# Turns one step later, finer steps beside the latent pieces, and a semaphore of its own for the high halves of the weight ring

## The chip, the cores and the metric

One NeuronCore of a Trainium2 chip runs the whole program. The metric is the device time of one execution in microseconds, the median of several runs. A text that gives a place in time gives it in us from the span's start in the profiled execution.

## The reference, cut to what matters

Two transformer blocks run one after the other over 256 tokens of width 2048, in float32.

```
first_block:
  n1 = rms_norm(x);  proj = n1 @ w_in            # q_lat 512, kv_lat 256, k_pe 64, q/k/v of the window attention
  q  = rms_norm(q_lat) @ w_q_b                   # 8 heads x (128 plain + 64 rotated columns)
  kv = rms_norm(kv_lat) @ w_kv_b                 # 8 heads x (128 key + 128 value columns)
  q, k = rms_norm per head, rope on the last 64; o_mla = causal softmax attention
  o_swa = window attention, 16 heads, bias table and a sink per head
  h = x + concat(rms_norm(o_mla), rms_norm(o_swa)) @ w_out
  h = h + peer(...)                              # routing over 16384 experts, peer_u, peer_v
second_block:
  proj = rms_norm(x) @ w_in_2                    # 6 x 1024 columns for two attentions, 4096 for gates
  oa = differential attention (4 heads), on = neighbourhood attention (8 heads, bias, 256 keys)
  x = x + rms_norm((g_a * oa @ w_a + g_b * on @ w_b) @ w_out)
  u = relu(rms_norm(x) @ w_up)^2                 # 2048 -> 8192
  x = x + rms_norm(u @ w_down)                   # 8192 -> 2048
```

## The kernel before, in words

**Pieces.** All weights come as 1101 pieces of 128 x 1024 float32 (512 KB), in the fixed order of the list `order`. SyncE's queue loads piece m into one of NR = 5 slots of `raw` (L2744). ScalarE writes its rounded high half to one of NH = 3 slots of `whi` (L1868), VectorE the rest to `wlo` (L2100). TensorE multiplies with high and low halves. A high slot may be overwritten when `piece_used` (s_used) says that TensorE is through with the whole piece, high and low products both; VectorE's low split waits for the high split alone and so for the same event through it. The split of piece n+2 is issued on both engines ahead of the products of piece n.

**Three forms of product.** `gemm` / `gemm_piece` (L340, L1655): 12 matmuls of 512 columns in a piece, weights moving: eight with `whi`, four with `wlo`. With `mid=True` the piece is cut into two halves of six, and a step (below) is taken between them. `gemm_rows` (L360, L1679) does the last three pieces of a product row block by row block. `gemm_wide` / `wide_piece` (L389, L1698), used by peer_w_q, peer_u and w_up: eight matmuls of 512 columns with `whi` stationary, then eight of 256 columns with `wlo`.

**Steps.** One Python program (`walk`) is run once for every engine and gives each engine its instructions in one fixed order. Side work (norms, rotations, turns by TensorE, attention units) stands in generators in `tasks` and `idle`; `step()` advances every one of them to its next `yield`. A generator that yields between two actions puts the second one behind the next piece, or half piece, on every engine. Each engine works strictly through its own order, so an instruction that waits holds up all behind it.

**Latent pieces.** After the fifth block of w_in come, in this order: `keys(0)`, `keys(1)` (one piece each), `swa_queries(1)` (eight pieces of w_in), `queries(2)` (the rotated part of q, two pieces), `values(0)`, `values(1)` (one each), `queries(0)`, `queries(1)` (two each). Their side work: `k_nope` (squares on ScalarE, `k_scale` and four `k_rows` on VectorE, turns, splits of the turned tile), `q_side` (norm of the window queries and their turns), `k_rope`, `q_nope`, `q_rope`, `q_scale`. `evac2` empties a product with half on ScalarE and half on VectorE. After `queries(1)` steps are taken with no product beside them until all turned tiles are split; then the scores of the latent attention start. GpSimd's order there: two fillings with zero for `k_rope` (L2680; the second waits for turns of the first), and, behind `queries(1)`, one small fill and eight writes of 2 MB that clear scr_g (L2694). Later in that order stands the reload of x into R (L2685), which the first residual behind w_out reads.

**Attention units.** `attend` is one unit: scores, yield, maximum and exponential, yield, turns of the exponentials (they wait for ScalarE's exponential, L1914), yield, copy, yield, product with the values, yield, finish. The window attention's 12 units run beside the first half of w_out, one started every second step, at half pieces; the neighbourhood attention's 8 units run beside the gate columns of w_in_2, two at a time, at whole pieces, and `finish_idle` behind the fifth gate product takes what steps are left over.

Of the kernel before, what the change touches and what calls it, by code (L numbers as in the profile page):

```python
# [37 lines left out]
def build(nc, D, out):  # L38
# [12 lines left out]
    with ExitStack() as ctx:  # L51
# [144 lines left out]
        s_hi, s_lo, s_used = sem("hi_split"), sem("lo_split"), sem("piece_used")  # L196
        s_vec = sem("vector_step")

        def walk(steps):
# [189 lines left out]
            def gemm_wide(name, units, both, toks, post, lead=2):  # L389
                taken = [take(accs) for _ in units]  # L390
                for c in range(4):
                    while len(toks) < min(2 * c + lead, 8):
                        step(0)
                    for n, (u, (pair, free)) in enumerate(zip(units, taken)):
                        i, low = piece(name, 4 * u + c)
                        high = fresh("PE", (s_hi, i + 1))
                        b = [banks[2 * pair], banks[2 * pair + 1]]
                        go("mm_wide", i, b, c, both, high, low, fresh("PE", toks[2 * c:2 * c + 2], free))
                        last = used_up()
                        if c == 3:  # L400
# [105 lines left out]
            def attend(scores, U, nk, scale, sink, pslots, blocks, pv, finish, combine=None, per_head=None, added=None):  # L506
# [30 lines left out]
                yield  # L537
# [227 lines left out]
            def swa_unit(t, h0):  # L765
# [20 lines left out]
                return attend(scores, U, nk, 1.0, sinks[:, h0:h0 + U], psw, 4, pv, finish, added=(of_head, bias_done[-1:]))  # L786
# [25 lines left out]
            def q_rope(ts, te, j):  # L812
                tr = []
                for t in range(2):
                    x = heads(ts[:, t, :], 8)
                    a = yield from squares(x, 8, ssq[:, 1, t, :], te)
                    t_ssq.append(a)
                    go("gain_rows", x, gq, 8, fresh("DVE", a, t_gr))
                    a = up("DVE", "gained")
                    yield  # L820
                    tr.append(rope(ts[:, t, :].rearrange("p (u c h) -> p u c h", u=8, c=2), 8, 32, CS[:, 0, t], CS[:, 1, t],
                                   [a, t_rope, x_read], Y[:, 0, 1024:2048]))
                    yield
# [6 lines left out]
            def q_scale():  # L830
                while len(t_ssq) < 6:
                    yield
                yield
# [51 lines left out]
            def keys(j):  # L885
                pair, b, last = gemm("w_kv_b", j, 2, BH[:, 4:6, :], BL[:, 4:6, :], nKV)
# [5 lines left out]
            def values(j):  # L892
                pair, b, last = gemm("w_kv_b", 2 + j, 2, BH[:, 4:6, :], BL[:, 4:6, :], nKV)
# [4 lines left out]
            def queries(j):  # L898
                pair, b, last = gemm("w_q_b", 2 * j, 4, BH, BL, nQ)
# [449 lines left out]
            def na_unit(h):  # L1349
# [16 lines left out]
                def masked_first():  # L1366
# [5 lines left out]
                                             masked))  # L1372
# [274 lines left out]
        def tensor_program(e):  # L1647
# [7 lines left out]
            def gemm_piece(i, b, c, n, lh, ll, high, low, free, kks=(0, 1)):  # L1655
# [5 lines left out]
                for kk in kks:  # L1661
                    kt = 2 * c + kk
                    w = slice(512 * kk, 512 * kk + 512)
                    for t in range(2):
                        a = slice(128 * t, 128 * t + 128)
                        mm(b[t][:, :], lh[:, kt, a], whi[:, s, w], kt == 0, False)
                        mm(b[t][:, :], ll[:, kt, a], whi[:, s, w], False, False)
# [11 lines left out]
            def gemm_rows(held, t, b, n, lh, ll, free):  # L1679
# [3 lines left out]
                for i, c, split in held:  # L1683
# [3 lines left out]
                    for kk in range(2):  # L1687
# [3 lines left out]
                        mm(b[t][:, :], lh[:, kt, a], wlo[:, s, w], False, False)  # L1691
                        last = mm(b[t][:, :], ll[:, kt, a], whi[:, s, w], False, kt == 2 * n - 1)
                    if t == 1:
                        last.then_inc(s_used, 1)
# [3 lines left out]
            def wide_piece(i, b, c, both, high, low, free):  # L1698
                s = i % NH
                for mark in free:  # L1700
                    e.wait_ge(*mark)
                for mark in high:
                    e.wait_ge(*mark)
                for kk in range(4):
                    kt = 4 * c + kk
                    x = both[:, kt, :, :].rearrange("p a n -> p (a n)")
                    for m in range(2):
                        w = slice(256 * kk + 128 * m, 256 * kk + 128 * m + 128)
# [1186 lines left out]
```

## Time and profile before

| | us |
|---|---|
| median of 3 runs | 3256.81 |
| lowest and highest | 3256.42 and 3257.52 |
| the profiled execution's own time | 3259.14 |
| its span, first to last instruction | 3257.3 |
| TensorE busy in matmuls | 3200.2 |
| VectorE busy | 2106.2 |
| ScalarE busy | 1517.7 |
| GpSimd busy | 492.0 |

Busy times are sums over the span. The granted clock of TensorE over the span was 0.994 of full. The profile's idle time before an instruction comes with what ended it; only waits on the chain to the end cost time.

### The profile page before, as it was taken

The numbers are of one execution on the slowest core, as the hardware profiler recorded it, in microseconds if no ns is written. First come the engines' busy times: TensorE is split into PE (matmuls) and PEld (weight loads), VectorE is DVE, ScalarE is ACT, GpSimd is POOL, SyncE is SP. The second block draws the span as 40 slices with busy tenths as digits, with TensorE's granted clock in tenths as the row PEclk, the third lists the DMA queues.
The fourth block names the chain that finished last, engine by engine and source line by source line (L and its number), as shares of the span: only waits on it lengthen the run. The fifth ranks groups of instructions, "written<-read, shape, count | busy, mean of one in ns | idle before, by whom it ended". The sixth has DMA issues, their size and how long they took to land.

```text
span 3257.3 us, 40800 instructions
## 1 busy us (share of the span) xinstructions
PE 3200.2 (98%) x16112; PEld 2715.7 (83%) x16112; DVE 2106.2 (65%) x3062; ACT 1517.7 (47%) x2006; POOL 492.0 (15%) x322
## 2 busy tenths in 40 slices
PE   8989999999999999999999999999999999999998
PEld 7788888888888888888888888888888788888886
DVE  6766578887555576666666565565465655655556
ACT  5645454545444444444444544445444544444443
POOL 1000005777777200000000000000000000000000
PEclk9999999999999999999999999999999999999999
DMA  8623557888888866666665555444555455555554
GB/s 321 252 85 130 181 183 208 214 214 215 212 214 211 262 249 244 250 248 245 245 233 200 197 184 174 165 170 176 191 194 188 174 192 191 193 189 193 189 192 149
DMA packets 220286, 660.95 MB, mean 203 GB/s; under 512 B 56704, under 2 KB 56848, under 8 KB 217536
## 3 DMA queue, kind: packets, MB, share of 16 engines
q1 hardware_dynamic: 170864, 600.81, 52.9%
q0 software_dynamic: 49232, 57.54, 8.7%
q8 instruction: 127, 2.08, 0.3%
q14 instruction: 63, 0.52, 0.0%
HBM read 622.48 MB, written 35.78 MB: 202 GB/s over the span
## 4 chain that ended last, share of the span: by engine, by line
PE 90%; DVE 6%; ACT 2%; issue 1%; DMA 1%; DVEq 0%; ACTq 0%; SPq 0%
PE PS L1649 89%; DVE wlo L2102 2%; PE PS L1723 2%; ACT whi L1872 1%; DMA raw<-in_w_in_b 0%; DVE R L2606 0%; ACT M L1914 0%; DVE AA L2148 0%; ACT Y L1958 0%; DVE TMP L2177 0%; DVE M L2507 0%; DVE TMP L2178 0%; DVE BB L2148 0%; DMA R<-in_x 0%; DMA M<-in_na_bias 0%
## 5 line engine op out<-in xcount | busy, mean ns | idle before, releaser
L2102 DVE TENSOR_TENSOR wlo<-raw,whi 128x1024 fp32r<-128x1024 f32 x1101 | 1343.8, 1224 | 889.6 <-ACT whi L1872 878.4
L1872 ACT ACTIVATE whi<-raw 128x1024 fp32r<-128x1024 f32 x1101 | 1157.8, 1057 | 1033.4 <-PE PS L1649 998.3
L1649 PE MATMUL PS<-whi,AA 128*128 128x512 f32 (+1 forms) x2880 | 718.7, 390 | 2.0 <-DVE AA L2148 1.2
L1649 PE MATMUL PS<-whi,BB 128*128 128x512 f32 x2640 | 667.4, 393 | 1.7 <-DVE wlo L2102 1.2
L1649 PEld LDWEIGHTS PS<-whi,AA 128*128 128x128 f32 x2880 | 537.0, 189 | 112.4 <-DVE AA L2148 2.0
L1649 PE MATMUL PS<-BB,whi 128*128 128x512 f32 x2304 | 577.4, 392 | 1.7 <-DVE BB L2148 1.7
L1649 PEld LDWEIGHTS PS<-whi,BB 128*128 128x128 f32 x2640 | 491.1, 188 | 102.3 <-DVE wlo L2102 1.8
L2699 POOL DMA_INDIRECT scr_g<-M x256 | 446.9, 1746 | 426.4 <-issue 390.2
L1649 PEld LDWEIGHTS PS<-BB,whi 128*128 128x128 f32 x2304 | 414.4, 189 | 76.1 <-DVE BB L2148 1.9
L1649 PE MATMUL PS<-wlo,AA 128*128 128x512 f32 (+1 forms) x1440 | 389.4, 388 | 1.9 <-DVE wlo L2102 1.9
L1649 PE MATMUL PS<-wlo,BB 128*128 128x512 f32 x1320 | 356.3, 389 | 0.5 <-DVE wlo L2102 0.5
L1649 PEld LDWEIGHTS PS<-BB,wlo 128*128 128x128 f32 x2304 | 314.3, 190 | 22.5
L1649 PE MATMUL PS<-BB,wlo 128*128 128x256 f32 x2304 | 321.2, 282 | 0.0
L1649 PEld LDWEIGHTS PS<-wlo,AA 128*128 128x128 f32 x1440 | 271.2, 188 | 58.0 <-DVE wlo L2102 2.3
L1649 PEld LDWEIGHTS PS<-wlo,BB 128*128 128x128 f32 x1320 | 247.7, 188 | 53.1 <-DVE wlo L2102 0.9
L1649 PE MATMUL PS<-AA,whi 128*128 128x512 f32 (+1 forms) x1056 | 263.8, 391 | 2.6 <-DVE AA L2148 2.2
L1649 PEld LDWEIGHTS PS<-AA,whi 128*128 128x128 f32 (+1 forms) x1056 | 189.4, 188 | 37.2 <-DVE AA L2148 2.8
L1649 PEld LDWEIGHTS PS<-AA,wlo 128*128 128x128 f32 (+1 forms) x1040 | 141.8, 189 | 10.0
L1649 PE MATMUL PS<-AA,wlo 128*128 128x256 f32 (+1 forms) x1040 | 147.2, 282 | 0.0
L1857 ACT ACTIVATE AA<-M 128x512 fp32r<-128x512 f32 x72 | 45.5, 632 | 150.8 <-DVE M L2507 143.8
L1857 ACT ACTIVATE M<-TMP 128x512 f32<-128x512 f32 x64 | 40.5, 633 | 128.1 <-DVE TMP L2498 100.5
L2708 POOL DMA_DIRECT2D M<-scr_a x16 | 8.8, 547 | 589.8 <-DVE AA L2514 543.6
(236 smaller groups left out, 1570.0 us busy)
## 6 DMA issues: line engine op xcount, KB each, us to landing
raw<-in_peer_u SPq DMA_DIRECT2D x256, 512.0 KB
raw<-in_peer_v SPq DMA_DIRECT2D x256, 512.0 KB
raw<-in_w_in SPq DMA_DIRECT2D x160, 512.0 KB
raw<-in_w_up SPq DMA_DIRECT2D x128, 512.0 KB
raw<-in_w_down SPq DMA_DIRECT2D x128, 512.0 KB
raw<-in_w_out SPq DMA_DIRECT2D x64, 512.0 KB
raw<-in_w_in_a SPq DMA_DIRECT2D x32, 512.0 KB
scr_g<-M POOLq DMA_DIRECT2D x8, 2048.0 KB, 30.1
```

The lines of the kernel that those rows point to most:

```text
L1649: return e.matmul(outp, l, r, start=start, stop=stop)
L1723: last = e.transpose(banks[bank][:, 128 * n:128 * n + 128], s, ident)
L1857: e.activation(o, x, func, **kw).then_inc(sem(name), 1)
L1872: e.activation(whi[:, n % NH, :], raw[:, n % NR, :], ACT.Copy).then_inc(s_hi, 1)
L2102: e.tensor_tensor(wlo[:, n % NH, :], raw[:, n % NR, :], bf(whi[:, n % NH, :]), ALU.subtract).then_inc(s_lo, 1)
L2699: e.indirect_dma_start(out=D["scr_g"].rearrange("e (t o) -> (e t) o", o=1), out_offset=bass.IndirectOffsetOnAxis(ap=EID[t][:, k:k + 1], ax ...
L2708: e.dma_start(glt[i], D["scr_a"][sc, :, :]).then_inc(sem(f"gelu_fetched{i}"), 16)
```

## The change

Five edits:

- The ring: a new semaphore `piece_hi_used` is raised at the last product with a high half. ScalarE's split of piece n now waits for it and for the low split of piece n-3 (which read that high half), no more for `piece_used`. VectorE's low split now waits for `piece_used` itself. In `gemm_rows`, `kpe_mm` and `sub_scores` the product with `wlo` becomes the last of its three.
- w_up alone, where one unit of 256 columns is computed at a time (60 pairs of pieces): two pieces are held, 16 high products and then 16 low ones. The first group, two units interleaved, stays at one piece.
- `keys`, `values`, `queries` use `mid=True`, so a step is also taken in the middle of each of their ten pieces.
- `q_rope`: both squares first, then both gains and both rotations in one step, and the turns in the next. `q_scale` waits for all turned q tiles.
- `slack=1` in the window and the neighbourhood attention: one more `yield` between the exponential and its turns.

```
-        s_hi, s_lo, s_used = sem("hi_split"), sem("lo_split"), sem("piece_used")
+        s_hi, s_lo = sem("hi_split"), sem("lo_split")
+        s_hi_used, s_used = sem("piece_hi_used"), sem("piece_used")
...
             def gemm_wide(name, units, both, toks, post, lead=2):
-                for c in range(4):
-                    while len(toks) < min(2 * c + lead, 8):
+                at_once = 2 if len(units) == 1 and name in ('w_up',) else 1
+                for c0 in range(0, 4, at_once):
+                    while len(toks) < min(2 * (c0 + at_once - 1) + lead, 8):
                         step(0)
                     for n, (u, (pair, free)) in enumerate(zip(units, taken)):
-                        i, low = piece(name, 4 * u + c)
-                        go("mm_wide", i, b, c, both, high, low, fresh("PE", toks[2 * c:2 * c + 2], free))
+                        held = []
+                        for c in range(c0, c0 + at_once):
+                            i, low = piece(name, 4 * u + c, NH - 1 - (c - c0))
+                            held.append((i, c, fresh("PE", (s_hi, i + 1)), low, fresh("PE", toks[2 * c:2 * c + 2], free)))
+                        go("mm_wide", held, [banks[2 * pair], banks[2 * pair + 1]], both)
+                        for _ in held[1:]:
+                            last = up("PE", "piece_used")
+                            step()
                         last = used_up()
...
-            def attend(..., per_head=None, added=None):
+            def attend(..., per_head=None, added=None, slack=0):
...
-                yield
+                for _ in range(1 + slack):
+                    yield
                 bank, bfree = yield from wait_for(misc)
                 tk = transposed(...)
...
             def q_rope(ts, te, j):
-                tr = []
+                xs, ta, tr = [heads(ts[:, t, :], 8) for t in range(2)], [], []
                 for t in range(2):
-                    x = heads(ts[:, t, :], 8)
-                    a = yield from squares(x, 8, ssq[:, 1, t, :], te)
-                    t_ssq.append(a)
-                    go("gain_rows", x, gq, 8, fresh("DVE", a, t_gr))
-                    a = up("DVE", "gained")
-                    yield
-                    tr.append(rope(...))
-                    yield
+                    ta.append((yield from squares(xs[t], 8, ssq[:, 1, t, :], te)))
+                t_ssq.extend(ta)
+                for t in range(2):
+                    go("gain_rows", xs[t], gq, 8, fresh("DVE", ta[t], t_gr))
+                    tr.append(up("DVE", "gained"))
+                for t in range(2):
+                    tr[t] = rope(...)
+                yield
...
             def q_scale():
-                while len(t_ssq) < 6:
-                    yield
-                yield
+                while len(t_ssq) < 6 or len(qt_done) < 6:
+                    yield
...
-                pair, b, last = gemm("w_kv_b", j, 2, BH[:, 4:6, :], BL[:, 4:6, :], nKV)
+                pair, b, last = gemm("w_kv_b", j, 2, BH[:, 4:6, :], BL[:, 4:6, :], nKV, mid=True)   # values, queries alike
...
             def split(n):                                   # ScalarE
                 if n >= NH:
-                    e.wait_ge(s_used, n - NH + 1)
+                    e.wait_ge(s_lo, n - NH + 1)
+                    e.wait_ge(s_hi_used, n - NH + 1)
...
             def split(n):                                   # VectorE
                 e.wait_ge(s_hi, n + 1)
+                if n >= NH:
+                    e.wait_ge(s_used, n - NH + 1)
```

## Rows read from the trace of the kernel before

**Rows 1.** The page's waits, whole span: engine, line, awaited; us in total, times, longest.

```profile
PE PS L1723 <- ACT M L1914: 8.6, 7, 2.9
```

**Rows 2.** Windows: stretch, busy time of the five engines, granted clock, DMA share, GB/s.

```profile
40.00:117.00 77.00, 73.26 (x356) 59.71 (x354) 55.91 (x114) 41.58 (x86) 9.05 (x8) 1.00 0.98 371
92.80:150.60 57.80, 55.50 (x257) 43.83 (x255) 46.45 (x97) 40.11 (x117) 1.12 (x1) 1.00 0.67 245
150.60:167.00 16.40, 6.48 (x33) 5.97 (x33) 13.95 (x35) 10.59 (x39) 0.95 (x1) 0.75 0.30 102
160.00:200.00 40.00, 35.80 (x284) 35.56 (x283) 24.67 (x56) 15.12 (x45) 0.00 (x0) 0.89 0.03 9
232.00:237.00 5.00, 5.00 (x19) 4.42 (x19) 4.89 (x18) 0.72 (x1) 0.00 (x0) 0.50 0.24 86
```

**Rows 3.** Groups of VectorE, 92 to 167 us: busy us, mean ns; idle before them.

```profile
L2102 DVE TENSOR_TENSOR wlo<-raw,whi 128x1024 fp32r<-128x1024 f32 x19 | 23.0, 1221 | 9.7 <-ACT whi L1872 9.7
L2190 DVE TENSOR_SCALAR M<-PS,ST 128x512 f32<-128x512 f32 x5 | 3.7, 746 | 0.1
```

**Rows 4.** Group of ScalarE, the same stretch and columns.

```profile
L1958 ACT ACTIVATE Y<-M 128x128 f32<-128x128 f32 (+1 forms) x50 | 13.8, 285 | 6.3 <-issue 6.3
```

**Rows 5.** Timeline of VectorE, 123 to 139 us: start, us, instructions, [idle before].

```profile
123.60 0.75 DVE L2190 TENSOR_SCALAR R<-PS,ST 128x512 f32<-128x512 f32 x1 [0.81 <-PE PS L1649]
...
138.44 0.75 DVE L2355 TENSOR_TENSOR M<-M,ST 128x256 f32<-128x256 f32 x2
```

**Rows 6.** Timeline of TensorE, 139 to 168 us.

```profile
139.25 0.66 PE L1723 MATMUL PS<-C,M 128*128 128x128 f32 x4 [0.37 <-DVE M L2355]
...
153.96 0.66 PE L1723 MATMUL PS<-C,M 128*128 128x128 f32 x4 [3.32 <-DVE M L2182]
...
157.02 5.78 PE L1723 MATMUL PS<-C,M 128*128 128x128 f32 x28 [2.40 <-DVE M L2355]
...
167.00 1.01 PE L1649 MATMUL PS<-BB,AA 128*128 128x256 f32 x3 [4.20 <-DVE AA L2148]
```

**Rows 7.** Timeline of GpSimd, 0 to 470 us.

```profile
39.93 8.00 POOL L2694 DMA_DIRECT2D scr_g<-M  x7 [0.30 <-POOL M L2688]
105.00 1.12 POOL L2694 DMA_DIRECT2D scr_g<-M  x1 [57.07 <-issue]
154.68 0.95 POOL L2680 MEMSET M<- 128x1024 f32 x1 [48.56 <-PE PS L1723]
212.57 0.73 POOL L2685 DMA_DIRECT2D R<-in_x  x1 [56.95 <-DVE AA L2148]
```

**Rows 8.** DMA issues, 200 to 240 us: count, KB each, us from issue to landing.

```profile
R<-in_x POOLq DMA_DIRECT2D x1, 2048.0 KB, 9.9
```

**Rows 9.** Timeline of VectorE, 231 to 234 us.

```profile
232.28 1.41 DVE L2373 SCALAR_TENSOR_TENSOR R<-PS,ST,R 128x512 f32<-128x512 f32 x2
```

**Rows 10.** TensorE's waits, 205 to 284 us (window attention).

```profile
PE PS L1723 <- ACT M L1914: 6.6, 4, 2.9
```

**Rows 11.** TensorE's waits, 2173 to 2280 us (neighbourhood attention), and its last turns.

```profile
PE PS L1723 <- ACT M L1914: 2.0, 3, 0.8
2278.62 0.60 PE L1723 MATMUL PS<-C,Y 128*128 128x128 f32 x4
```

**Rows 12.** TensorE's waits, 2535 to 2553 us (start of w_up); ScalarE's timeline there.

```profile
PE PS L1723 <- DVE R L2606: 1.3, 2, 0.9
PE PS L1649 <- DVE AA L2148: 0.4, 1, 0.4
2547.39 1.06 ACT L1872 ACTIVATE whi<-raw 128x1024 fp32r<-128x1024 f32 x1 [1.72 <-PE PS L1649]
```

**Rows 13.** Timeline of TensorE: a piece of w_up, then a part of one of w_down.

```profile
2707.28 2.00 PE L1649 MATMUL PS<-AA,whi 128*128 128x512 f32 x8
2709.12 1.11 PE L1649 MATMUL PS<-AA,wlo 128*128 128x256 f32 x8
...
3227.47 1.98 PE L1649 MATMUL PS<-whi,BB 128*128 128x512 f32 x8
```

More of the change, by code:

```diff
@@ L504, in walk, with attend @@
             alt = [0]
-            def attend(scores, U, nk, scale, sink, pslots, blocks, pv, finish, combine=None, per_head=None, added=None):
+            def attend(scores, U, nk, scale, sink, pslots, blocks, pv, finish, combine=None, per_head=None, added=None, slack=0):
                 bank, bfree = yield from wait_for(misc)
@@ L898, in queries @@
             def queries(j):
-                pair, b, last = gemm("w_q_b", 2 * j, 4, BH, BL, nQ)
+                pair, b, last = gemm("w_q_b", 2 * j, 4, BH, BL, nQ, mid=True)
                 ts, free = take(qrows)
@@ L1696, in gemm_rows, with wide_pieces @@
                     last.then_inc(sem("rows_done"), 1)
[L1698 to L1708, printed above, removed]
-                        mm(b[m][:, :], whi[:, s, w], x, kt == 0, False)
-                for mark in low:
-                    e.wait_ge(*mark)
-                for kk in range(4):
-                    kt = 4 * c + kk
-                    for m in range(2):
-                        w = slice(256 * kk + 128 * m, 256 * kk + 128 * m + 128)
-                        last = mm(b[m][:, 0:256], wlo[:, s, w], both[:, kt, 0, :], False, kt == 15)
-                last.then_inc(s_used, 1)
+            def wide_pieces(held, b, both):
+                for i, c, high, low, free in held:
+                    for mark in free:
+                        e.wait_ge(*mark)
+                    for mark in high:
+                        e.wait_ge(*mark)
+                    for kk in range(4):
+                        kt = 4 * c + kk
+                        x = both[:, kt, :, :].rearrange("p a n -> p (a n)")
+                        for m in range(2):
+                            w = slice(256 * kk + 128 * m, 256 * kk + 128 * m + 128)
+                            last = mm(b[m][:, :], whi[:, i % NH, w], x, kt == 0, False)
+                    last.then_inc(s_hi_used, 1)
+                for i, c, high, low, free in held:
+                    for mark in low:
+                        e.wait_ge(*mark)
+                    for kk in range(4):
+                        kt = 4 * c + kk
+                        for m in range(2):
+                            w = slice(256 * kk + 128 * m, 256 * kk + 128 * m + 128)
+                            last = mm(b[m][:, 0:256], wlo[:, i % NH, w], both[:, kt, 0, :], False, kt == 15)
+                    last.then_inc(s_used, 1)
             def transpose(srcs, bank, ready):
@@ L1742, in kpe_mm @@
                     mm(o, whi[:, s, w], AH[:, kt, :], kt == 0, False)
-                    mm(o, wlo[:, s, w], AH[:, kt, :], False, False)
-                    last = mm(o, whi[:, s, w], AL[:, kt, :], False, kt == 15)
+                    high = mm(o, whi[:, s, w], AL[:, kt, :], False, False)
+                    last = mm(o, wlo[:, s, w], AH[:, kt, :], False, kt == 15)
+                high.then_inc(s_hi_used, 1)
                 last.then_inc(s_used, 1)
@@ L1812, in sub_scores @@
                     mm(o, AH[:, hp, a], whi[:, s, w], True, False)
-                    mm(o, AH[:, hp, a], wlo[:, s, w], False, False)
-                    last = mm(o, AL[:, hp, a], whi[:, s, w], False, True)
+                    high = mm(o, AL[:, hp, a], whi[:, s, w], False, False)
+                    last = mm(o, AH[:, hp, a], wlo[:, s, w], False, True)
+                if end:
+                    high.then_inc(s_hi_used, 1)
                 last.then_inc(s_used if end else sem("sub_scores"), 1)
```

25 lines of the change are left out of this document (13 added, 12 removed).

## The prediction

> **What bounds the kernel now.** I read the page's busy times first: TensorE 3200 of 3257 us, so all its idle time together is 57 us, and no cut in the other engines' work counts unless TensorE waits for it there. Then the page's waits: the largest that this change touches is TensorE's turns waiting for ScalarE's exponentials, 8.6 us in all [rows 1]. Then windows, to see which stretch is dense. In 92.8 to 150.6 us TensorE is busy 55.5 of 57.8 us, in 150.6 to 167.0 only 6.48 of 16.4 [rows 2]: 12.2 us idle in the latent stage, the largest hole near the changed lines. VectorE is busy 46.45 + 13.95 = 60.4 of those 74.2 us, and 9.7 of the other 13.8 are waits of the low split for the high split [rows 3]; it has about 4 us of slack of its own. The clock belongs to the picture: it was granted 1.00 up to 150.6, 0.75 behind, and exactly half (1.2 of 2.4 GHz) in 232 to 237 [rows 2], behind a wait of 2.9 us [rows 10], so a hole costs more than its length. Last, the waits of each later stretch one by one.
>
> **1. Steps in the middle of the ten latent pieces, and q_rope's new order.** The products are the same; ten more steps draw the side work ahead. VectorE's order up to `head_scale` hardly shrinks: before it ran from the evacuation of the last window query product at 123.60 to `head_scale` at 138.44 [rows 5], 14.8 us, with TensorE's turns right behind at 139.25, having waited 0.37 [rows 6]. In the new order I count between the same two, by durations of this stretch: two evacuations .75 + .7 [rows 3], two low splits at 1.15 net of overlap, two gain-and-rope groups 2.1, x's low halves 1.7, the head sums 1.15, the root 2.1, the spread .75, the scale 1.15, and 1.05 of waiting: 13.7 us. It starts later, at 124.4 instead of 123.3, because both turn groups of the keys now stand behind one half piece and wait for all four `k_rows` (+1.1). So the scaled tile is there at 138.1. TensorE's work up to the turns is now two pieces (5.5), turns (.95) and one of values (2.75), which ends at 133.5: it waits 4.6.
>
> Then the q turns. `q_rope` gave them six steps behind the first squares; now both rotations stand in one step and the turns in the next, half a piece on. VectorE has to do a low split (1.15) that waits for ScalarE's squares (1.9; 16 of the groups of .28 [rows 4] beside evacuations) and high split (1.06), with 1.85 idle, then gains 1.3 and rotations 4.4: done at 147.6. TensorE is there at 140.5: it waits 7.1. The next spread and the k turns cost 2.7, and the drain before the latent scores keeps its 4.2 [rows 6]. Sum of waits 1.1 + 4.6 + 7.1 + 2.7 + 4.2 = 19.7 against 12.2 now: **+7.5**, the half clock of the holes taken as hidden in the waits for VectorE. Bounds: if VectorE's total is the only limit, holes move and none is added (0, and -2 if the earlier work thins the drain); if each of the new holes drops the clock as that of 2.9 us did, five us at half rate more, +12.
>
> The order also moves GpSimd. Its second zero fill was issued at 154.68, behind clears issued from 39.93 on, the last at 105.00 after 57 us in the queue [rows 7]. In the new walk the second fill, which waits for turns, is emitted ahead of the clears. So the eight writes leave near 155. In 40 to 117 us the DMA engines were busy .98 at 371 GB/s; in 160 to 200, .03 [rows 2]. Early pieces land sooner, worth 0.3 us by the one wait there (range 0 to 0.5): **-0.3**. But the reload of x was issued at 212.57 [rows 7] and took 9.9 us [rows 8] with the queue empty; the first scaled residual reads it at 232.28 [rows 9]. The clears took 77 us beside the weight pieces (39.9 to 117); with nearly nothing beside them I take 65 to 70, ending near 225, and the reload near 234, about when it is needed: **+0.5**, range 0 to 9.
>
> **2. One more step in the window attention.** Queued behind a waiting turn is all of TensorE's order. In 205 to 284 us TensorE waits 6.6 us for exponentials in four places [rows 10]. Half a piece (1.5 us) more between them: the three short ones vanish, the longest shrinks to nothing as well, as the units start every second step and the turns then fall on the other one. A wait of .8 for a low split there goes too. The half clock in 232 to 237 [rows 2] did 5 us in what full clock does in 2.5; its cause is that wait, so 2.6 come back. At the end of the half the pipeline drains one step later: the residual's 1.4 [rows 9] and a step without product, +1.8. Sum -6.6 - .8 - 2.6 + 1.8 = **-8.2**; range -6 (clock falls elsewhere) to -11 (drain hidden).
>
> **3. One more step in the neighbourhood attention.** Three waits, 2.0 us [rows 11], vanish behind a whole piece. A pair of units takes 8 steps instead of 7; over four pairs the last turns (now at 2278.62, .60 for a group) fall into the steps behind the fifth gate product. They are the same work in another place, with nothing late in front: **-2.0**, range -2.0 to 0 (two more unproductive steps of copies and exponentials).
>
> **4. The ring's semaphore.** In steady stages TensorE does not wait for splits at all, so there it is worth 0. It tells where VectorE is late. At the start of w_up ScalarE's high split begins at 2547.39, 1.72 idle, released by TensorE's last product of the older piece [rows 12]; with high products first that event comes some .95 us earlier. VectorE's low split then is done before the norm's turns need VectorE, and the waits of 1.3 + .4 [rows 12] go: **-1.7**, range 0 to -2.2. The added wait stands on VectorE's low split for `piece_used`; ahead of it was the same event by way of ScalarE, so nothing behind it comes later. The other added wait, ScalarE's for the low split of three pieces ago, is long met.
>
> **5. Pairs in w_up.** 60 pairs, the same matmuls, half the changes of form. Eight high products run from 2707.28 to 2709.12 in w_up, 1.84 us, against 1.81 for the same in w_down (3227.47 to 3229.28) [rows 13]. The .03 fits a cost of changing form; of it I take .02 a pair: 60 x .02 = **-1.2**, range -1.8 to 0 (a gain for nothing else would need a wait, and there is none). A pair holds two slots of `whi` of three: the third is split while 16 high products run (3.7 us against 1.06), so it costs nothing; with that cover gone it would be 1 us a pair.
>
> [...]
>
> **Sum.** -0.3 + 7.5 + 0.5 - 8.2 - 2.0 - 1.7 - 1.2 = -5.4. The profiled execution took 3259.1 (span 3257.3); its change is laid on the median, 2.3 us lower: 3256.8 - 5.4 = **3251.4**.
>
> **The rivals.**
>
> A. The latent stage loses nothing. For it: VectorE is the bound there (60.4 busy of 74.2), its work is the same, and TensorE's finer steps may only trade the final 4.2 and the 3.32 for waits ahead. Against: VectorE's idle time behind the high split (9.7) grows if ScalarE does squares first. Time: 3256.8 - 5.4 - 7.5 = 3243.9.
>
> B. Slower than before, by one mechanism: the reload of x behind the clears. If these keep the 77 us that they took, 155 + 2 + 77 = 234, the reload lands at 244, 9 us behind the first residual at some 235; VectorE stands, TensorE's next split stands, and the clock falls for 5 us (2.6 to 3.4). Price 12.4 in place of .5: 3251.4 + 11.9 = 3263.3. It decides from a landing at about 241, where the sum passes 0. Against: fewer other transfers than in 40 to 117, where pieces of 512 KB shared the engines.
>
> C. The ring and the pairs do nothing, which is what they say only on paper: TensorE never waits for either in steady state. Without the 1.7 and the 1.2: 3254.3.
>
> **How the numbers follow.** Forecast .50, A .30, B .10, C .10. A measurement of this kernel tells 0.2% (6.5 us) from no change, so the bounds are 3250.3 and 3263.3. The forecast's own spread, 3247 to 3257, lies for a third beyond 3250.3; A all; C none; B half above 3263.3, to which I add the upper ends of the latent term. Faster .30 + .17 = .47, slower .09, same .44. Range: A with its latent -2 at 3242 below, above the forecast with its latent term at +12 and a small share of B, 3260.
>
> **What would show it.** Right: TensorE's latent scores start at about 173 instead of 167.0, with a wait of some 7 us for the rotations in the middle of values(1) and one of 4 to 5 for the scale near 134; GpSimd's clears issued behind 155 and a DMA share near 1 until 225; no wait for exponentials in 205 to 284 and 2173 to 2280, granted clock 1.0 at 232 to 237; 16 high products of w_up in about 3.66 us; no waits at 2540 to 2551. Wrong: latent scores at or before 167 (A), the first residual waiting for x (B), any steady stage with waits for `whi` or `wlo`.

## The result, and the profile after

| | before | after |
|---|---|---|
| median | 3257.2 us (8 runs) | 3269.5 us (8 runs) |
| lowest and highest | 3256.4 and 3263.0 | 3263.7 and 3270.9 |
| profiled execution, its span | 3259.1, 3257.3 | 3267.9, 3266.0 |

Ratio 1.0032, 95% interval 1.0024 to 1.0041: slower by some 12 us where 5.4 us less were forecast. The profiled execution is one of the milder ones, 8.7 us over that of before.

The page of the changed kernel, busy times (part 1) and the chain of waits by engine (part 4):

```profile
PE 3200.5 (98%) x16112; PEld 2719.2 (83%) x16112; DVE 2093.6 (64%) x3062; ACT 1519.2 (47%) x2006; POOL 526.8 (16%) x322
...
PE 72%; POOL 14%; issue 4%; DVE 4%; DMA 3%; ACT 2%; DVEq 0%; ACTq 0%; SPq 0%; POOLq 0%
```

TensorE and ScalarE have their old sums. GpSimd has 35 us more (492.0 before), with the same number of instructions, and it stands in the chain to the end with 14%. The prediction says nothing of what this engine does behind the reload of x.

TensorE's waits over the whole span (line and awaited; us, times, longest). Lines have moved: the turns are L1734 (L1723 before), the products L1655 (L1649).

```profile
PE PS L1655 <- DVE AA L2165: 9.5, 5, 5.6
PE PS L1655 <- ACT whi L1887: 7.4, 3, 6.9
...
PE PS L1734 <- DVE M L2199: 5.7, 1, 5.7
...
PE PS L1734 <- DVE R L2183: 4.2, 1, 4.2
PE PS L1655 <- ACT PTb L1871: 3.8, 1, 3.8
PE PS L1734 <- DVE M L2372: 2.6, 1, 2.6
```

The exponentials of [rows 1] (8.6 us) are gone from the list altogether. New are the high split (6.9 at once), the rotations (5.7), the scale (4.2) and a copy by ScalarE (3.8). Their places, in TensorE's timeline:

```profile
133.40 1.97 PE L1734 MATMUL PS<-C,R 128*128 128x128 f32 x8 [4.19 <-DVE R L2183]
...
143.06 1.11 PE L1734 MATMUL PS<-C,M 128*128 128x128 f32 x4 [5.75 <-DVE M L2199]
...
158.94 0.66 PE L1734 MATMUL PS<-C,M 128*128 128x128 f32 x4 [2.56 <-DVE M L2372]
...
171.71 1.01 PE L1655 MATMUL PS<-BB,AA 128*128 128x256 f32 x3 [5.59 <-DVE AA L2165]
...
238.59 1.76 PE L1655 MATMUL PS<-M,PTb 128*128 128x64 f32 x8 [3.76 <-ACT PTb L1871]
...
1156.98 3.70 PE L1655 MATMUL PS<-BB,whi 128*128 128x512 f32 x8 [6.94 <-ACT whi L1887]
```

The first four answer to [rows 6]: the latent scores start at 171.7 instead of 167.0. The last stands at a piece of peer_u, the fifth from its end, where before TensorE had no wait at all. What held it, from the waits of 1140 to 1165 us:

```profile
DVE M L2524 <- DMA M<-scr_g: 10.1, 1, 10.1
```

VectorE stood 10.1 us for the gate values' load from scr_g, which it multiplies into peer_v's first operand. ScalarE's rounding of that operand waited for VectorE, and the high split of a piece of peer_u stood behind it on ScalarE:

```profile
1155.35 0.63 ACT L1871 ACTIVATE AA<-M 128x512 fp32r<-128x512 f32 x1 [12.11 <-DVE M L2524]
1155.88 1.04 ACT L1887 ACTIVATE whi<-raw 128x1024 fp32r<-128x1024 f32 x1
```

The load could only be issued when GpSimd had written all gate values into scr_g, 256 indirect writes. Windows (busy time of the five engines, granted clock, DMA share, GB/s), the first around that wait, the second to be held against the fourth of [rows 2]:

```profile
1150.00:1160.00 10.00, 3.06 (x8) 2.45 (x8) 3.95 (x7) 2.72 (x4) 0.00 (x0) 0.68 0.87 318
...
160.00:200.00 40.00, 34.41 (x257) 33.20 (x256) 21.42 (x49) 17.55 (x62) 3.18 (x3) 0.87 1.01 350
```

With the wait of 6.9 and the half clock behind it, VectorE's low split of the next piece comes 16.0 us later than before (1156.96 against 1140.93), where the last one ahead of the wait came 5.9 later (1143.27 against 1137.39): 10.1 us. The third column of the table below has the same 10 us. GpSimd's timeline has the clears where they were forecast, and the reload waiting behind them:

```profile
155.20 7.98 POOL L2711 DMA_DIRECT2D scr_g<-M  x7 [0.30 <-POOL M L2705]
207.44 1.12 POOL L2711 DMA_DIRECT2D scr_g<-M  x1 [44.26 <-issue]
218.34 0.72 POOL L2702 DMA_DIRECT2D R<-in_x  x1 [9.77 <-DMA scr_g<-M]
```

Lengths of four stretches, from TensorE's timelines, in us: from the start to the latent scores; from there to the wait at peer_w_q's start; from there to the norm ahead of w_up; and w_up and w_down, from w_up's first product to the wait at 3236.8 of before (the norm's 9 us between the last two are left out; they are the same in all). Each row is one profiled execution. The first column varies by up to 1.6 us between kernels that are the same up to that point (164.8 to 166.4 in experiments 6, 9 to 12 and 14).

| | to the scores | window attention | peer, second block | w_up, w_down |
|---|---|---|---|---|
| before | 167.0 | 181.2 | 2173.9 | 705.2 |
| after | 171.7 | 182.4 | 2179.7 | 702.2 |
| ring alone | 165.5 | 180.8 | 2173.0 | 704.2 |
| old ring in peer_u | 170.8 | 185.8 | 2169.6 | 703.1 |
| the same, early clears | 172.6 | 179.4 | 2169.6 | 703.0 |
| the same, latent edits undone | 165.6 | 180.0 | 2169.6 | 703.1 |

### The profile page after: what moved, and what is told of

Read it like the earlier page. It is cut to its first block, busy times and chain, and to the rows that moved or that the text cites. A ratio compares the mean times of both kernels' runs of the same rounds, so it can differ in the third digit from the quotient of the medians.

```text
span 3266.0 us, 41894 instructions
## 1 busy us (share of the span) xinstructions
PE 3200.5 (98%) x16112; PEld 2719.2 (83%) x16112; DVE 2093.6 (64%) x3062; ACT 1519.2 (47%) x2006; POOL 526.8 (16%) x322
## 4 chain that ended last, share of the span: by engine, by line
PE 72%; POOL 14%; issue 4%; DVE 4%; DMA 3%; ACT 2%; DVEq 0%; ACTq 0%; SPq 0%; POOLq 0%
PE PS L1655 71%; POOL scr_g L2716 14%; DMA scr_g<-M 2%; PE PS L1734 1%; DVE wlo L2119 1%; ACT whi L1887 1%; ACT M L1929 0%; DMA M<-scr_g 0%; ACT Y L1973 0%; DVE R L2623 0%; DVE M L2228 0%; DVE AA L2165 0%; DMA TMP<-in_key_pos 0%; DVE M L2524 0%; DMA R<-in_x 0%
## 5 line engine op out<-in xcount | busy, mean ns | idle before, releaser
L1655 PE MATMUL PS<-whi,AA 128*128 128x512 f32 (+1 forms) x2880 | 719.9, 390 | 2.1 <-DVE AA L2165 1.2
L1655 PE MATMUL PS<-whi,BB 128*128 128x512 f32 x2640 | 670.8, 394 | 1.2 <-DVE wlo L2119 1.2
L1655 PEld LDWEIGHTS PS<-whi,AA 128*128 128x128 f32 x2880 | 536.8, 189 | 111.5 <-DVE AA L2165 2.0
L1655 PE MATMUL PS<-BB,whi 128*128 128x512 f32 x2304 | 579.2, 393 | 8.9 <-ACT whi L1887 7.2
L1655 PEld LDWEIGHTS PS<-whi,BB 128*128 128x128 f32 x2640 | 493.1, 189 | 101.9 <-DVE wlo L2119 1.6
L2716 POOL DMA_INDIRECT scr_g<-M x256 | 481.7, 1882 | 438.9 <-issue 394.6
L1655 PEld LDWEIGHTS PS<-BB,whi 128*128 128x128 f32 x2304 | 415.4, 189 | 83.9 <-ACT whi L1887 7.6
L1655 PE MATMUL PS<-wlo,AA 128*128 128x512 f32 (+1 forms) x1440 | 388.7, 387 | 0.0
L1655 PE MATMUL PS<-wlo,BB 128*128 128x512 f32 x1320 | 359.1, 390 | 0.0
L1655 PEld LDWEIGHTS PS<-BB,wlo 128*128 128x128 f32 x2304 | 314.4, 190 | 22.5
L1655 PE MATMUL PS<-BB,wlo 128*128 128x256 f32 x2304 | 321.2, 282 | 0.0
L1655 PEld LDWEIGHTS PS<-wlo,AA 128*128 128x128 f32 x1440 | 271.1, 188 | 55.8
L1655 PEld LDWEIGHTS PS<-wlo,BB 128*128 128x128 f32 x1320 | 248.5, 188 | 52.5
L1655 PE MATMUL PS<-AA,whi 128*128 128x512 f32 (+1 forms) x1056 | 252.1, 389 | 1.8 <-DVE AA L2165 1.8
L1655 PEld LDWEIGHTS PS<-AA,whi 128*128 128x128 f32 (+1 forms) x1056 | 193.3, 188 | 39.2 <-DVE AA L2165 2.2
L1655 PEld LDWEIGHTS PS<-AA,wlo 128*128 128x128 f32 (+1 forms) x1040 | 133.9, 190 | 5.3
L1655 PE MATMUL PS<-AA,wlo 128*128 128x256 f32 (+1 forms) x1040 | 137.9, 282 | 0.0
L2382 DVE TENSOR_TENSOR R<-R,PS 128x512 f32<-128x512 f32 x128 | 82.1, 683 | 46.4 <-PE PS L1655 46.3
```

Of the source, the lines that this page charges most:

```text
L1655: return e.matmul(outp, l, r, start=start, stop=stop)
L2382: last = e.tensor_tensor(R[:, t, c], R[:, t, c], b[t][:, :], ALU.add)
L2716: e.indirect_dma_start(out=D["scr_g"].rearrange("e (t o) -> (e t) o", o=1), out_offset=bass.IndirectOffsetOnAxis(ap=EID[t][:, k:k + 1], ax ...
```

## Why GpSimd's writes took longer

The 256 indirect writes run from 515.0 to 1086.5 us before (571) and from 520.9 to 1139.7 after (619). VectorE's first use of the load that follows stands at 1138.5 before and would have stood at 1144.5 after. Before, GpSimd's load and VectorE's first use; then the load after:

```profile
1090.50 0.97 POOL L2709 DMA_DIRECT2D M<-scr_g  x1
...
1138.53 0.76 DVE L2507 TENSOR_TENSOR M<-M 128x256 f32<-128x256 f32 x2
```

```profile
1144.04 0.97 POOL L2726 DMA_DIRECT2D M<-scr_g  x1
```

From the end of the last write to the gate values in place are 14.9 us after (1139.7 to 1154.55). So by my estimate the chain before could have ended 37 us later at no cost (1138.5 - 14.9 - 1086.5). It ended 53 us later, with 6 of them allowed for by the later deadline: 10 too many. The 53 are 35 us of longer writes, some 12 of longer gaps between them and 6 of a later start.

The lengthening is nearly all in the later part: the first 124 writes take 291 us before and 295 after, at 1.85 us a write in both, the other 132 take 280 and 324. Why the first part is slow with the old ring too was not measured; VectorE has about three times as many instructions there. Groups of the writes between 820 and 1140 us (busy us, mean ns | idle before), first before, then after:

```profile
L2699 POOL DMA_INDIRECT scr_g<-M x126 | 206.8, 1641 | 61.3 <-issue 44.6 <-DMA scr_g<-M 16.8
```

```profile
L2716 POOL DMA_INDIRECT scr_g<-M x130 | 248.6, 1912 | 71.5 <-issue 47.4 <-DMA scr_g<-M 24.1
```

One write became .27 us dearer. Single ones show how. Before, GpSimd and then VectorE in peer_u:

```profile
900.59 1.58 POOL L2699 DMA_INDIRECT scr_g<-M  x1 [0.30 <-issue]
902.48 1.55 POOL L2699 DMA_INDIRECT scr_g<-M  x1 [0.30 <-issue]
...
899.53 1.23 DVE L2102 TENSOR_TENSOR wlo<-raw,whi 128x1024 fp32r<-128x1024 f32 x1 [0.89 <-ACT whi L1872]
...
902.75 1.23 DVE L2102 TENSOR_TENSOR wlo<-raw,whi 128x1024 fp32r<-128x1024 f32 x1 [0.26 <-ACT whi L1872]
```

After, the same two engines:

```profile
920.45 1.99 POOL L2716 DMA_INDIRECT scr_g<-M  x1 [0.30 <-issue]
922.75 1.73 POOL L2716 DMA_INDIRECT scr_g<-M  x1 [0.30 <-issue]
924.79 2.57 POOL L2716 DMA_INDIRECT scr_g<-M  x1 [0.30 <-issue]
...
919.80 1.22 DVE L2119 TENSOR_TENSOR wlo<-raw,whi 128x1024 fp32r<-128x1024 f32 x1 [0.26 <-ACT whi L1887]
...
922.38 0.68 DVE L2515 TENSOR_TENSOR TMP<-TMP,PTb 128x512 f32<-128x512 f32 x1
...
924.72 1.22 DVE L2119 TENSOR_TENSOR wlo<-raw,whi 128x1024 fp32r<-128x1024 f32 x1 [1.65 <-ACT whi L1887]
```

A write that starts while VectorE is idle takes 1.55 us, also when VectorE starts an operation during it (902.48). One that starts inside an operation of VectorE with both sources in SBUF is prolonged by what is left of that operation less some .13 us: 924.79 starts with 1.15 left and takes 2.57, 1.02 more; 922.75 with .31 left, .18 more. Over all writes behind 820 us, counted in the trace: before, 53 of 125 start inside such an operation and cost .23 us more on the mean; after, 99 of 129, at .48 us. The others cost 0 to .02 more in both.

It is a rhythm. Two pieces of peer_u last 5.58 us, and three undisturbed writes with their gaps of .30 last 5.55: before, six writes fall into four pieces, and the few hundredths that are missing come from starting in the last .17 us of a split. After, five writes (1.99 + 1.73 + 2.57 + 1.81 + 1.54 and five gaps, 11.2 us) take the time of four pieces. What moved is VectorE: ScalarE's high split no longer waits for the low products of the old piece (.94 us of TensorE), so three low splits of four stand .94 us earlier in the piece's time.

The Trainium skill, "SBUF — State Buffer", section "SBUF: two separate sides", says that an operation of VectorE with two SBUF sources and an instruction of GpSimd that reads SBUF exclude each other, the later one waiting for the first to end. The rows agree for a write that comes second (1.02 us more with 1.15 left). They do not for the other order: 150 low splits before and 140 after start inside a write, and all take 1.20 to 1.23 us, the others 1.20 to 1.29. In these rows only GpSimd waits; why is open.

## The experiments

Each was timed in three rounds beside the kernel before, whose median in these sessions was 3258.1 to 3258.5.

**1. The ring alone.** The changed kernel with all other edits undone; what is left is the diff of the two splits' waits, the order of products in three functions and the new semaphore.

> The kernel before with the ring's semaphores alone (products in the new order, w_up still piece by piece, no other edit). Theory R (the ring moves VectorE's low splits in peer_u by some .9 us on two pieces of four, and GpSimd's indirect writes lock into starting inside them): the 256 indirect writes take about 615 us instead of 571, the last ends some 15 us short of the deadline or later (after 1125), TensorE waits up to 7 us near 1144, and the time is 3256.8 - 1.7 (w_up's start) + 6 to 10 = 3261 to 3265. Theory P (only the phase in which the upstream changes leave GpSimd against VectorE decides): the writes take 571 us as before, no wait near 1144, the time is 3255.1.

Median 3263.8: two runs at 3253.8 and 3255.2, eight at 3263.1 to 3265.8. The profile fell on the run of 3255.2; its chain of writes ends at 1119.0, GpSimd 475.8 us busy in it (446.9 before), without a wait near 1150. So the ring alone lengthens the chain, by 35 us here, and gains some 3 us elsewhere. In this run the load was issued at 1124.2 and first used at 1136.6, 12.4 us later, where the changed kernel needed 10.5 from issue to use: some 2 us were in hand. That the upper group is the late load was open and led to experiment 13.

**2. The old ring, all else changed.**

```
                 if n >= NH:
-                    e.wait_ge(s_lo, n - NH + 1)
-                    e.wait_ge(s_hi_used, n - NH + 1)
+                    e.wait_ge(s_used, n - NH + 1)       # ScalarE; VectorE's own wait for s_used taken out
```

> The changed kernel with the old waits of the two splits (both by way of piece_used), all else as changed. Theory R: the indirect writes take about 571 us, the wait of 7 us at 1150 and its half clock (10.1 together) are gone, w_up's start gives 1.7 back: 3269.5 - 10.1 - 1.6 (the median lies above the profiled run) + 1.7 = about 3259.5. Theory P: the writes still take over 600 us and the time stays at 3268 to 3272.

Median 3263.3 (3258.9 to 3264.1), chain from 524.0 to 1099.2 (575 us), no wait near 1150. The mechanism is as theory R has it; the time is 3.8 us above its number. Part of that may be a wait of TensorE near 208 us with half clock behind it (3.2 us here, 2.65 and 2.8 in experiments 3 and 4), which the changed kernel's profile did not have; how much of it was not measured.

**3. The old ring for peer_u's pieces alone.** The same diff under `if order[n][0] == 'peer_u'`.

> The changed kernel with the old waits for the pieces of peer_u alone. Theory R: as with the old ring, and w_up's 1.7 us stay: about 3257.8, no wait near 1150, the writes in about 571 us. Theory P: 3268 to 3272, the writes over 600 us. If the clears of scr_g that run later were the cause (theory C), no change either.

Median 3259.5 (3257.3 to 3261.1), 1.7 above the forecast of theory R and 10.0 us better than the changed kernel by one condition on 256 pieces. The chain ends at 1100.4. Its writes between 820 and 1140 us:

```profile
L2718 POOL DMA_INDIRECT scr_g<-M x132 | 212.3, 1608 | 70.8 <-issue 50.1 <-DMA scr_g<-M 20.7
```

**4. A quarter of the writes left out,** the ring as changed.

```
-                    for k in range(16):
+                    for k in range(12):
                         go("gate_scatter", t, 16 * h + k, ...)
```

> The changed kernel with 12 of the 16 indirect writes of each round (a quarter of the scatter is left out of the computation). All theories that put the 10.1 us on the end of the chain of indirect writes: that chain ends near 990, TensorE's wait near 1150 is gone, the time is 3269.5 - 10.1 - 1.6 = about 3257.8, and its spread over runs falls to about 1 us. If something else held peer_v's first tile (the fetch of scr_a, the queue of loads), the wait stays and the time too.

Median 3259.5 (3257.6 to 3261.0), chain's end at 978.4. Two ways to get the chain done in time, the rhythm and the number of writes, give the same time: the late end of the chain costs the 10.0 us, and the slow rhythm by itself nothing. The spread was 3.4 us and not the 1 that was expected, so it has another source.

**5. The clears back at 40 us,** on the base of experiment 3.

```
+            go("gate_blank")                # and the eight gate_clear
             keys(0)
...
-            go("gate_blank")                # and the eight gate_clear
             while len(qt_done) < 6 or len(kt_done) < 8 or not t_rq:
```

> Base: the changed kernel with the old ring waits in peer_u (3259.5). Here its eight clears of scr_g (and their small fill) are also put ahead of keys(0) in GpSimd's order, so that they run from about 40 us on as before the change. Theory K (the clears at 155 to 220 slow the load of the key positions, behind which TensorE waits 2.8 us at 207 and then works at half clock until about 219): the load lands 3 to 4 us sooner, the wait shrinks to below 1 us, no half clock there, the time is 3259.5 - 3.5 = 3256.0 (3253 to 3257.5), and the runs lie within 2 us of one another. Rival: the clears only fill an empty stretch, the time stays at 3259.5; or their early run slows the pieces of w_in more than the base shows, then up to +1.

Median 3257.0 (3255.4 to 3258.7), 2.5 us better, where 3.5 were expected. The spread is still 3.3 us, not below 2: the clears are not its source, and what is was not found. In the base VectorE waits for the key positions, and the clock falls behind it; timeline of VectorE and a window of the base, then the same window here:

```profile
208.76 1.28 DVE L2269 SCALAR_TENSOR_TENSOR Y<-POS,C,R 128x1024 f32<-128x1024 int32 x1 [2.21 <-DMA R<-in_key_pos]
...
210.00:217.00 7.00, 6.90 (x33) 6.90 (x34) 4.51 (x8) 0.00 (x0) 0.14 (x1) 0.50 0.90 311
```

```profile
210.00:217.00 7.00, 6.61 (x50) 6.07 (x49) 6.86 (x13) 2.66 (x6) 0.00 (x0) 1.00 0.01 5
```

50 matmuls instead of 33 in the same 7 us. The stretch shrinks from 185.8 to 179.4 us, and 1.8 us of it are paid back ahead of the scores (170.8 to 172.6), where the clears again delay the early pieces; by the spread of that column the 1.8 may be little more than chance. In the profile of the changed kernel TensorE's waits there were .7 and 1.1 us, with the clears as late: the long wait comes in some executions and not in others.

**6. The latent edits undone,** on the same base: `q_rope`, `q_scale` and whole pieces as before. The clears go back by themselves.

> The same base with q_rope, q_scale and the latent pieces (no half pieces) as before the change. The clears then return to 40 us by themselves. If the latent edits cost what the two profiles say (latent scores at 167.0 against 171.7) and the clears 3.5: 3259.5 - 4.7 - 3.5 = 3251.3. Rival (the finer steps' loss is repaid later, since the window attention starts with more done): 3256.

Median 3250.4 (3249.4 to 3251.5), ratio to before .9976, interval .9966 to .9987: faster than both kernels. From experiment 5 to this one are 6.6 us, the price of the latent edits; the scores start at 165.6 instead of 172.6.

**7 and 8. One half of the latent edits each.** In 7 `mid=True` is taken from the ten pieces, in 8 `q_rope` and `q_scale` are as before.

> The same base with the ten latent pieces whole again, q_rope and q_scale as changed. Theory M (the half pieces make TensorE reach the turns before VectorE is through, 4.3 and 5.9 us of wait at 129 and 137): both waits shrink to below 1 us, the latent scores start at 167 to 168 and the time is about 3251 to 3253, the clears going back to 40 us too. Theory Q (q_rope's new order, both rotations in one step, makes the wait of 5.9): that wait stays at 4 us or more, the time is 3255 to 3257.

> The same base with q_rope and q_scale as before, the latent pieces in halves as changed. Theory M: the scale's wait of 4.3 at 129 stays, the scores start at 170 to 172 and the time within 1 us of 3259.5. Theory Q: the wait of 5.9 at 137 goes and nothing takes its place, the scores start at 167, the time is near 3254.

Experiment 7: 3252.8 (3251.3 to 3254.3); experiment 8: 3258.1 (3255.0 to 3264.2, two of ten above 3262). TensorE's timeline, first 7, then 8:

```profile
146.86 1.12 PE L1734 MATMUL PS<-C,M 128*128 128x128 f32 x4 [8.00 <-DVE M L2201]
```

```profile
145.83 0.66 PE L1735 MATMUL PS<-C,M 128*128 128x128 f32 x4 [4.08 <-DVE M L2202]
...
171.76 1.01 PE L1656 MATMUL PS<-BB,AA 128*128 128x256 f32 x3 [7.96 <-DVE AA L2168]
```

Both theories have a part and neither its picture. With whole pieces and the new q_rope the wait for the rotations grows to 8.0 us, but the one for the scale (4.2) goes and the last shrinks to 1.84: the scores start at 170.2 and 2.7 us of it come back in the window attention (177.3). With half pieces and the old q_rope one wait of 4.1 and a last one of 8.0 remain. Against the base of experiment 6, the new q_rope alone costs 2.4 us (3252.8 against 3250.4); the half pieces and the clears that move with them cost 7.7 (3258.1), of which 2.5 are the clears' by experiment 5.

**9. The window attention's extra step taken back,** on the base of 6 (3250.4), as in 10 to 12.

```
-                return attend(..., added=(of_head, bias_done[-1:]), slack=1)
+                return attend(..., added=(of_head, bias_done[-1:]))
```

> Base: the changed kernel with the old ring waits in peer_u and the latent edits undone (3250.4). Here the window attention has its old order (no extra step between exponential and turns). The prediction's step (8.2 us for this edit) would give 3258.6. Theory W (the waits for exponentials went, but one wait of 3.75 us behind the two squares of the latent output on ScalarE, with its half clock, took the place of the old one, and 1.9 us of drain were added): the stretch between latent scores and peer_w_q was 181.2 before and is 180.0 in the base, so the edit is worth about 1: 3251.4.

3251.5 (3249.4 to 3251.7): the edit is worth 1.1 us, if anything; the forecast had 8.2. TensorE's longest wait is again that of before:

```profile
230.91 1.12 PE L1735 MATMUL PS<-C,M 128*128 128x128 f32 x4 [2.85 <-ACT M L1932]
```

**10. The neighbourhood attention's extra step taken back,** `slack=1` out of its call.

> The same base with the neighbourhood attention in its old order. The prediction's step (2.0 us) gives 3252.4. By the stage lengths of the profiles (2169.6 us from peer_w_q to the norm ahead of w_up in the base, 2173.0 with the ring alone) it is 3.4: 3253.8. Rival: that difference is the ring's old waits in peer_u or drift, then 3250.4.

3252.6 (3251.2 to 3254.1), 2.2 us: near the 2.0 of the prediction, below the 3.4 by stage lengths. The waits of [rows 11] are back:

```profile
PE PS L1735 <- ACT M L1932: 1.7, 3, 0.8
```

**11. w_up piece by piece,** `at_once = 1`.

> The same base, w_up piece by piece. The prediction's step (60 pairs by .02) and the stage lengths (703.1 us in the base, 704.2 with the ring alone): 1.1 to 1.2 us, 3251.5. If spacing follows from columns alone: 3250.4.

3251.6 (nine runs of 3250.9 to 3252.5; the tenth took 5613.6), 1.2 us, and the stretch is 704.4 instead of 703.1. In all profiles with the new ring it is 704.2 to 704.5 without pairs (three kernels) and 702.2 to 703.5 with them. The pairs in the changed kernel's timeline:

```profile
2702.90 3.82 PE L1655 MATMUL PS<-AA,whi 128*128 128x512 f32 x16
2706.56 2.08 PE L1655 MATMUL PS<-AA,wlo 128*128 128x256 f32 x16
```

From start to start 3.66 us for 16 high products, where twice [rows 13] is 3.68.

**12. The two squares a step earlier.**

```
-            r_om, t_om = row_factor(OM, list(om_done.values()), 5)
+            r_om, t_om = row_factor(OM, list(om_done.values()), 4)
```

> The same base, the two squares of the latent output's norm (2.2 us on ScalarE) four steps behind the attention's start instead of five, so that they fall into a step in which no unit has its exponentials. Theory W: the wait of 3.75 us near 229 and its half clock (2.5 us) are gone: 3250.4 - 6.3 = 3244.1. Rival (VectorE's maxima and low splits are the bound there, the wait turns up a step on): 3249 to 3251.

3251.0 (nine runs of 3249.9 to 3251.8; the tenth took 4573.6): nothing gained, the rival holds. TensorE:

```profile
230.75 1.10 PE L1656 MATMUL PS<-M,PTb 128*128 128x64 f32 x8 [2.76 <-ACT PTb L1872]
238.28 1.10 PE L1656 MATMUL PS<-M,PTb 128*128 128x64 f32 x8 [2.07 <-DVE PTb L2256]
```

The one wait of 3.75 became two, 4.8 together, and small ones behind. The granted clock stayed 1.00 over 222 to 240 us, and yet the stretch is 182.0 long, against 180.0. Theory W had the place of the wait right and the cause only in part.

**13. The ring alone, a quarter of the writes left out** (the diffs of 1 and 4 together).

> The kernel with the ring's semaphores alone (3263.8, its runs in two groups, at 3254 to 3255 and at 3263 to 3266), here with 12 of the 16 indirect writes of each round (a quarter of the scatter is left out of the computation). If the upper group comes from the chain of indirect writes ending behind peer_v's first tile: one group remains, at 3253 to 3256. If it comes from anything else in the ring (a stall that the one profile of that kernel missed): both groups stay and the median is 3263 to 3264.

3255.6, all ten runs in 3254.6 to 3256.2. The upper group is gone: it was the chain. With that the ring, by itself, is worth 2.5 us against the 3258.1 of before in that session; the interval of the ratio, .9982 to 1.0002, just includes no gain.

**14. The base of 6 with the new ring in peer_u too.**

> The changed kernel with the latent edits undone, the ring's new waits everywhere, peer_u too; against 3250.4 with the old waits in peer_u. Theory R: GpSimd's writes lock into VectorE's splits again, the chain takes 606 to 619 us and ends within 15 us of the deadline or behind it: most runs at 3256 to 3260, some near 3250. If the latent edits were needed for the lock (theory P, the phase): 3250 to 3251, all runs.

3259.7: two runs at 3249.0 and 3249.3, eight at 3259.2 to 3261.2. Against 3250.4 one condition on peer_u's pieces decides 10 us in eight runs of ten. The profile is of the lower group, with the chain from 511.1 to 1117.1, 606 us. Its row answers to the two above:

```profile
L2717 POOL DMA_INDIRECT scr_g<-M x124 | 233.0, 1879 | 64.9 <-issue 41.8 <-DMA scr_g<-M 23.2
```

So the slow rhythm (1.88 to 1.91 us a write against 1.59 to 1.64) belongs to the ring, with or without the latent edits. Whether a run pays depends on whether the load lands in time: here it was issued at 1122.3 and first used at 1134.9, again some 2 us more than the 10.5 that it took in the changed kernel.

## Why the prediction was wrong

**Part 4 failed, and with it the sign.** It said of the ring's semaphore that in steady stages TensorE does not wait for splits, "so there it is worth 0". True of TensorE, and wrong as a sum: the waits shift VectorE's splits within each piece, and GpSimd pays for it write by write, until its chain ends 10 us too late for the load behind peer_v's first operand. +10.0 us by experiments 3 and 4. I had asked what is queued behind the added wait and not who shares a resource with the instruction that moves. That "nothing behind it comes later" was true as well, and did not help: three splits of four come .94 us earlier. The rows to see it in were in the trace of before: 256 writes whose duration varies between 1.55 and 2.57 us, and a chain that ends 52 us ahead of the first use of its result, some 15 of them taken by landing and load. Rival B had the right sign by the wrong transfer, and C, which called the ring without effect in steady state, shared the mistake.

**The ring's gain** was forecast at 1.7 and only at w_up's start; it is 2.5 (experiment 13). The waits of [rows 12] did go, but w_up and w_down became only 1.0 shorter (705.2 to 704.2); of the rest .9 lies in the stretch ahead of them (2173.9 to 2173.0).

**Latent pieces: right.** Forecast were waits of 4.6, 7.1, 2.7 and 4.2 and scores at 173; the waits are 4.2, 5.8, 2.6 and 5.6, the scores at 171.7 (172.6 with the clears in their old place). +7.5 forecast, 6.6 measured (experiments 5 and 6). The closeness is in part luck: the sum set new waits (19.7) against the old idle time (12.2), of which [rows 6] have 10.3 as waits, and one wait came out 1.3 shorter and another 1.4 longer than forecast. Its start, 123.3, stands at 123.60 in [rows 5], which changes nothing.

**The clears: right in place, undersized.** They run from 155 on, and the early pieces gain at most 1.8 us (.3 forecast), by one profile each. The reload of x was awaited by nobody: issued at 218.3, and with the 9.8 us that it takes, in place at 228, ten ahead of the residual at 238.6. That part of rival B fell. Not foreseen was the load of key positions on SyncE's queue, with its wait and the half clock behind. Net the later clears lose 2.5 us instead of .2 (experiment 5).

**Window attention: wrong by 7 us.** Forecast -8.2, measured -1.1 (experiment 9). The four waits did go. But the sum counted the removed waits and their half clock and no new one. In their place stand one wait of 3.75 us and the half clock behind it, and the drain of 1.9 (1.8 forecast). What is late there is ScalarE: two squares of 2.2 us in the same step as a unit's exponentials, then the high split, for which VectorE waits 4.4 us with the next maxima behind. That "the longest shrinks to nothing as well" was said of one wait alone, and no other engine was walked through that step. Experiment 12 shows that moving the squares is no cure; what bounds the stretch there in full was not settled.

**Neighbourhood attention and pairs: right.** -2.0 and -1.2 forecast, 2.2 and 1.2 measured. If the spacing of matmuls followed from their columns alone, the pairs would have given 0; experiment 11 gives 1.2, at the edge of what ten runs can tell, with the stretch of the profiles on its side.

**The sum by measurement:** +10.0 + 2.5 + 6.6 - 1.1 - 2.2 - 1.2 - 2.5 = +12.1, against 12.3 between the medians. It proves less than it seems to: the 10.0, 2.5 and 6.6 are steps from the changed kernel down to experiment 6 and add up by construction, so only the other four are tested, 7.0 us against the 7.8 between before and experiment 6. The changed kernel was timed in the first session alone, where before took 3257.2 and not 3258.1 to 3258.5, so the 10.0 are uncertain by 1 us, and each part by its spread of 2 to 4. Not settled is why the times with the new ring fall into two groups 9 to 10 us apart and not into a band: only the changed kernel's own profile shows a run with the wait. The 2 us in hand in the lower group (experiments 1 and 14) say why small shifts decide, not why the step is so large.

**The version that beats both:** all edits except the latent ones, and the old ring waits for peer_u's pieces: 3250.4, 7.8 us below the kernel before in the same session (3258.2) and 19 below the changed one in its own. What it keeps are the pairs, the two extra steps and the ring outside peer_u.

## What to carry to other kernels

When a wait is added or taken away, look at every engine that shares a resource with the instruction whose time moves, and at the slack of its longest chain, however far its deadline; here some 37 us of slack behind a chain of 571 went mostly by .27 us an instruction. When steps are made finer beside an engine that is nearly full, TensorE arrives sooner and the tile does not. When a wait is counted as gone, walk the other engines through the new order as far as the next two waits: here 1.1 us came of the 8.2 forecast.

## What the runs showed of the hardware

GpSimd's indirect writes take 1.55 us, and up to 2.57 when issued inside VectorE's subtraction of two SBUF tiles; VectorE's operation keeps its 1.22 to 1.23 us in both cases. The two then fall into a fixed rhythm, six or five writes to four pieces, that lasts, with short breaks, for over 200 us. The loads of key positions, 512 KB on SyncE's queue, landed in 3.8 and 5.1 us before (medians of two) and in 8.5 and 9.3 us under the clears' traffic in the changed kernel (155 to 225 us, DMA share mostly 1). TensorE's clock fell to half behind waits of 2.65 (experiment 3), 2.9 and 3.75 us, and stayed full over waits of 2.76 and 2.07 us that stood 7.5 us apart (experiment 12): the length of a wait alone does not tell.
